# A gated linear recurrence (RG-LRU): gates computed as tanh, one logarithm per pair of tiles, element-wise work begun two projection units earlier

## The chip, the core and the metric

The kernel runs on one core of one Trainium2 chip. The metric is the device time of one execution in microseconds (us). The kernel before takes 1957.4 us, the median of three runs (1946.94 to 1958.04).

## What is computed

The program computes two blocks of a network on a sequence of 256 tokens of width 1024. The first block has two layers, each a mixer and a gated feed-forward part with norms around them; the second block (two layers of attention and delta rule) comes after and is not touched but for the name of one semaphore. The change lies in the second mixer of the first block, a gated linear recurrence of width 1280 (10 heads of 128):

```
proj = u @ w_in + b_in
ybr  = gelu(proj[:, :1280])                      # the y half
xbr  = causal_dwconv(proj[:, 1280:])             # the x half, 4 taps
gx   = sigmoid(xbr @ w_gx + b_gx)                # per head
ga   = sigmoid(xbr @ w_ga + b_ga)
log_a = -8 * softplus(-lam) * ga
a    = exp(log_a)
h_t  = a_t * h_{t-1} + sqrt(1 - a_t^2) * (gx * xbr)_t
m    = (h * ybr) @ w_out + b_out
```

## The kernel before

Everything is held transposed: features in 128 partitions, the 256 tokens along the free axis, so that a tile is 128x256. All large weights come as one stream of chunks of 128x2048 numbers (1 MB each), loaded by SyncE into a ring of three buffers `raw`. Each chunk is split before use: ScalarE copies it in two halves of 1024 columns into `w_hi` (rounded), and VectorE writes the remainder `w_lo = raw - w_hi`, also in halves. The two buffers of `w_hi` and `w_lo` alternate, so chunk c+2 can be split only while chunk c is being used up; the helper `ahead(split, engine, c)` splits chunk c+2 (`act_split` and `act_half` on ScalarE, `dve_split` and `dve_half` on VectorE). TensorE makes three products for every tile of weights (lines 521 to 523: hi with hi, hi with lo, lo with hi).

Two kinds of chunk matter here. `pe_unit` uses one of kind a: 48 matmuls that write one "unit", two output tiles, into one of the two PSUM banks `unit`. `pe_down` uses one of kind b: 48 matmuls that add a pair of input tiles (split into `mv_hi` by ScalarE, line 575, and `mv_lo` by VectorE, line 579) into the eight tiles of `acc`.

The mixer is a hand-written order of instructions on three engines, joined by semaphores. Stage `lru_in` has 10 chunks (c0 to c0+9): units 0 to 4 give the x half, units 5 to 9 the y half. Stage `lru_out` has five (c0+10 to c0+14), one "down" for each pair of tiles.

- TensorE (`pe_lru`): units 0 to 4; then five times the gate products of two heads (line 1184, into `misc`) and one more unit; then three small products (`pe_mod`, and `pe_ada` for blocks 18 and 19); then `pe_out`, the five downs. Down j waits for `mv_lo` of pair j.
- ScalarE (`act_lru`): copies units 0 to 4 out with the bias (line 1224), then per pair of heads two sigmoids each (lines 1236 and 1237) and a tanh each (line 1242, with a scale per feature), and copies out a unit of the y half (line 1248). When all gates are read it loads a table, takes the gelu of eight tiles at once (line 1252), loads the table of logarithm and exponential (line 1253), and for every pair q takes two logarithms (lines 1264 and 1265), two exponentials for a (line 1267) and `mult(q)`, the exponential of half the difference (line 1258). Since t = tanh(log a), the identity is 1 - a^2 = -2t/(1 - t): hence two logarithms. Then it loads the gelu table again, takes the gelu of the last unit from PSUM (line 1276), and makes the first two `mv_hi` (`act_lead`); `act_out` goes on with the splits and the later `mv_hi`.
- VectorE (`dve_lru`): four taps per tile of the x half (lines 1295 to 1298, each linked to the one before), the product gx*x (line 1305), `diff(q)` (line 1314, the difference of the logarithms), and `recur(q)`: sqrt(1-a^2)*gx*x (line 1321), two scans (line 1323), and the product with the y half (line 1331). `diff(0)`, `diff(1)`, a split, `recur(0)`, `diff(2)`, `recur(1)`, `diff(3)`, `diff(4)` come before the first `mv_lo`; then per down one split, one `recur`, one `mv_lo`. At the end `dve_mod`, two `dve_ada`, and the bias on the eight tiles of the result (line 1350), which the next norm reads.

GpSimd only issues DMAs in this kernel.

## Time and profile before

| | before |
|---|---|
| median of three runs | 1957.4 us |
| the profiled execution | 1948.02 us |
| its span, first to last instruction | 1945.9 us |
| mean granted TensorE clock | 0.967 |
| TensorE / VectorE / ScalarE busy | 94% / 67% / 53% |
| TensorE idle before the first down of `lru_out` | 18.25 us |

All rows below are of that one profiled execution, and times in them are from the start of its span; 2.1 us of the execution lie around the span. `lru_in` runs from 573 us to 642 us, `lru_out` from 663 us to 697 us. Busy time of TensorE counts pipelined matmuls, whose records overlap.

### The profile page before, as it was taken

The numbers are of one execution on the slowest core, as the hardware profiler recorded it, in microseconds if no ns is written. First come the engines' busy times: TensorE is split into PE (matmuls) and PEld (weight loads), VectorE is DVE, ScalarE is ACT, GpSimd is POOL, SyncE is SP. The second block draws the span as 40 slices with busy tenths as digits, with TensorE's granted clock in tenths as the row PEclk, the third lists the DMA queues.
The fourth block names the chain that finished last, engine by engine and source line by source line (L and its number), as shares of the span: only waits on it lengthen the run. The fifth ranks groups of instructions, "written<-read, shape, count | busy, mean of one in ns | idle before, by whom it ended". The sixth has DMA issues, their size and how long they took to land. (4 is left out here: it accounts for less than half of the span.)

```text
span 1945.9 us, 40030 instructions
## 1 busy us (share of the span) xinstructions
PE 1822.1 (94%) x16281; PEld 1727.0 (89%) x16281; DVE 1294.4 (67%) x1994; ACT 1026.0 (53%) x1550; POOL 29.5 (2%) x48
## 2 busy tenths in 40 slices
PE   6999999999989689999979999889998999988999
PEld 5996889999969579999969999889998999988999
DVE  5947667777657477777766866665556776766555
ACT  5644555555556655555546555344444665444443
POOL 0000000000000000000000001000000000100000
PEclk9999899999989799999989999989998999999999
DMA  7540446777754345666733340335553433044553
GB/s 287 191 154 1 170 176 247 271 260 258 269 211 159 145 173 207 225 237 226 269 108 130 135 169 24 109 109 195 195 194 124 159 133 128 3 147 141 192 193 129
DMA packets 43887, 333.54 MB, mean 171 GB/s; under 512 B 4864, under 2 KB 4992, under 8 KB 5632
## 3 DMA queue, kind: packets, MB, share of 16 engines
q1 hardware_dynamic: 38592, 277.89, 39.5%
q0 software_dynamic: 4608, 50.33, 6.9%
q10 hardware_dynamic: 576, 3.71, 0.5%
q8 instruction: 85, 1.39, 0.3%
q14 instruction: 26, 0.21, 0.0%
HBM read 330.86 MB, written 1.05 MB: 171 GB/s over the span
## 5 line engine op out<-in xcount | busy, mean ns | idle before, releaser
L501 DVE TENSOR_TENSOR w_lo<-raw,w_hi 128x1024 fp32r<-128x1024 f32 x526 | 640.5, 1224 | 435.0 <-ACT w_hi L492 425.3
L492 ACT ACTIVATE w_hi<-raw 128x1024 fp32r<-128x1024 f32 x526 | 555.4, 1061 | 615.6 <-PE unit L523 374.6
L521 PE MATMUL unit<-h_hi,w_hi 128*128 128x256 f32 x2656 | 752.7, 283 | 40.9 <-DVE h_lo L426 28.2
L522 PE MATMUL unit<-h_lo,w_hi 128*128 128x256 f32 x2656 | 745.1, 281 | 0.0
L523 PE MATMUL unit<-h_hi,w_lo 128*128 128x256 f32 x2656 | 744.9, 280 | 0.0
L521 PEld LDWEIGHTS unit<-h_hi,w_hi 128*128 128x128 f32 x2656 | 508.6, 191 | 52.5 <-issue 36.2
L522 PEld LDWEIGHTS unit<-h_lo,w_hi 128*128 128x128 f32 x2656 | 508.8, 192 | 0.2
L523 PEld LDWEIGHTS unit<-h_hi,w_lo 128*128 128x128 f32 x2656 | 508.5, 191 | 0.0
L521 PE MATMUL acc<-mv_hi,w_hi 128*128 128x256 f32 x1360 | 384.4, 283 | 33.4 <-DVE mv_lo L579 33.4
L522 PE MATMUL acc<-mv_lo,w_hi 128*128 128x256 f32 x1360 | 380.8, 280 | 0.0
L523 PE MATMUL acc<-mv_hi,w_lo 128*128 128x256 f32 x1360 | 380.6, 280 | 0.0
L521 PEld LDWEIGHTS acc<-mv_hi,w_hi 128*128 128x128 f32 x1360 | 261.0, 192 | 49.6 <-DVE mv_lo L579 35.8
L522 PEld LDWEIGHTS acc<-mv_lo,w_hi 128*128 128x128 f32 x1360 | 260.8, 192 | 0.0
L523 PEld LDWEIGHTS acc<-mv_hi,w_lo 128*128 128x128 f32 x1360 | 260.5, 192 | 0.0
L575 ACT ACTIVATE mv_hi<-keep 128x512 fp32r<-128x512 f32 x93 | 57.4, 621 | 41.0 <-DVE keep L977 13.5
L579 DVE TENSOR_TENSOR mv_lo<-keep,mv_hi 128x512 fp32r<-128x512 f32 x93 | 63.6, 687 | 14.9 <-ACT mv_hi L575 14.7
L406 PE MATMUL misc<-h,con 128*128 128x256 f32 x180 | 50.2, 440 | 19.7 <-ACT h L387 19.5
L406 PEld LDWEIGHTS misc<-h,con 128*128 128x128 f32 x180 | 39.2, 223 | 29.8 <-ACT h L387 12.9
L1035 ACT ACTIVATE keep<-unit,par 128x256 f32<-128x256 f32 x128 | 64.3, 552 | 0.0
L1089 DVE SCALAR_TENSOR_TENSOR keep<-unit,par,keep 128x254 f32<-128x254 f32 x128 | 55.8, 477 | 8.4
L1084 DVE SCALAR_TENSOR_TENSOR keep<-unit,par,keep 128x255 f32<-128x255 f32 x128 | 55.8, 477 | 5.6 <-ACT keep L1035 2.8
L1719 DVE SCALAR_TENSOR_TENSOR tmp<-unit,par,tmp 128x255 f32<-128x255 f32 (+1 forms) x96 | 41.9, 478 | 4.2 <-ACT tmp L1602 2.8
(375 smaller groups left out, 1711.1 us busy)
## 6 DMA issues: line engine op xcount, KB each, us to landing
raw<-w_in SPq DMA_DIRECT2D x263, 1024.0 KB, 4.8
ada_ring<-ada_in POOLq DMA_DIRECT2D x32, 1536.0 KB, 7.6
keep<-gates_in ACTq DMA_DIRECT2D x1, 1280.0 KB, 7.2
par<-par_in ACTq DMA_DIRECT2D x1, 1261.0 KB, 14.6
x<-x_in SPq DMA_DIRECT2D x1, 1024.0 KB, 5.6
out<-x SPq DMA_DIRECT2D x4, 256.0 KB, 2.1
con<-con_in ACTq DMA_DIRECT2D x1, 950.0 KB, 5.0
con<-con_in ACTq DMA_DIRECT2D x1, 130.0 KB, 5.8
```

Of the source, the lines that this page charges most:

```text
L406: last = mm(misc[0][:, 0:T], ones, h[:, t, :], start=(t == 2 * order[0]), stop=(t == 7))
L492: act(half(w_hi, c, k), raw[c % RAW][:, CW // 2 * k:CW // 2 * (k + 1)], ACT.Copy).then_inc(S("high_parts"), 1)
L501: tt(half(w_lo, c, k), raw[c % RAW][:, CW // 2 * k:CW // 2 * (k + 1)], half(w_hi, c, k).bitcast(f32), ALU.subtract).then_inc(S("chunk_spli ...
L521: mm(out, w, m, start=first, stop=False)
L522: mm(out, w, ml, start=False, stop=False)
L523: return mm(out, wl, m, start=False, stop=last)
L575: act(mv_hi[:, b % 2, :, :], src, ACT.Copy).then_inc(S("mv_hi_done"), 1)
L579: tt(mv_lo[:, b % 2, :, :], src, mv_hi[:, b % 2, :, :].bitcast(f32), ALU.subtract).then_inc(S("mv_ready"), 1)
L1035: ins = act(fc[:, s], unit[u % 2][:, s], ACT.Identity, bias=column(u, 4 * side + 3, i), scale=column(u, 4 * side + 2, i))
L1084: ins = stt(fc[:, o + 1:o + T], src[:, o:o + T - 1], column(u, 4 * side + 1, i), fc[:, o + 1:o + T], ALU.mult, ALU.add)
L1089: ins = stt(fc[:, o + 2:o + T], src[:, o:o + T - 2], column(u, 4 * side, i), fc[:, o + 2:o + T], ALU.mult, ALU.add)
L1719: ins = stt(dst, src[:, a:z], pr("dn_conv", 60 * l + 5 * t + tap), dst, ALU.mult, ALU.add)
```

## The change

1. TensorE issues the gate products one unit earlier: the first pair of heads after unit 3 and not after unit 4, so that two units (8 and 9) stand behind the last gate products where one stood.
2. The gates are computed as tanh(x/2) with half the bias, sigmoid being (1 + tanh(x/2))/2. VectorE makes (1 + t)*x in one instruction (line 1321 of the new kernel) and z = log a = c*t + c in another, new one (line 1324), both in the old place of the product gx*x. The factor 2 that is left over is taken back in the scale of the logarithm.
3. ScalarE takes tanh of z for a pair at once (line 1249), a = exp(z) for a pair at once (line 1253), and only one logarithm for a pair (line 1258). VectorE squares a (line 1347) and multiplies (a^2 + 1) with tanh(z) (line 1348): `square_gap(q)` in place of `diff(q)`. 1 - a^2 = -(1 + a^2)*tanh(log a).
4. No table load stands between tanh and gelu in the new program, and units 5 to 7 take their gelu while they are copied from PSUM (line 1235). Units 8 and 9 are copied plain, and one gelu over four tiles follows later (line 1299). The program has three table loads in this mixer where it had five.
5. Before the first down only pairs 0 to 2 have `square_gap`, and only `recur(0)` is done; `square_gap(3)` and `(4)` stand behind downs 0 and 1. The halves of a chunk's `w_lo` are made on either side of `mv_lo`. VectorE's split of chunk c0+15 is moved ahead of `dve_mod`.
6. Three semaphores of the second block become one (same waits).

```diff
-            for j in range(1, 5):
+            for j in range(1, 4):
                 pe_unit(pe, c0 + j, n0 + j)
...
             for k in range(5):
                 gates(2 * k)
                 gates(2 * k + 1)
-                pe_unit(pe, c0 + 5 + k, n0 + 5 + k)
+                pe_unit(pe, c0 + 4 + k, n0 + 4 + k)
+            pe_unit(pe, c0 + 9, n0 + 9)
...
+            def gate_in(n, func):
+                done_after(ac, c0 + n)
+                for e in range(2):
+                    j = 2 * (n - 5) + e
+                    ins = act(R["yb"][:, j, :], unit[n % 2][:, T * e:T * (e + 1)], func, bias=pr("lru_b_in", j))
+                ins.then_inc(S("unit_free"), 1)
...
-                    act(R["gx"][:, j % 3, :], misc[j % 2][:, 0:T], ACT.Sigmoid, bias=pr("b_gx", j))
-                    act(ga_(j)[:, 0, :], misc[j % 2][:, T:2 * T], ACT.Sigmoid,
-                        bias=pr("b_ga", j)).then_inc(S("lru_gate_read"), 1)
+                    act(R["gx"][:, j % 3, :], misc[j % 2][:, 0:T], ACT.Tanh, scale=0.5, bias=cv[0][:, j:j + 1])
+                    act(ga_(j)[:, 0, :], misc[j % 2][:, T:2 * T], ACT.Tanh, scale=0.5, bias=cv[1][:, j:j + 1]
+                        ).then_inc(S("lru_gate_read"), 1)
...
+            def tanh_z(q):
+                ac.wait_ge(S("lru_z"), 2 * q + 2)
+                act(w_(2 * q, 2), ga_(2 * q, 2), ACT.Tanh).then_inc(S("lru_tanh"), 1)
+
+            def decay(q):
+                ac.wait_ge(S("lru_tanh"), q + 1)
+                act(ga_(2 * q, 2), ga_(2 * q, 2), ACT.Exp).then_inc(S("lru_a"), 1)
+
+            def mult(q):
+                ac.wait_ge(S("lru_diff"), q + 1)
+                p = lg[:, 2 * q:2 * q + 2, :]
+                link(act(p, p, ACT.Ln, scale=-0.25, bias=one("tiny")))
+                act(p, p, ACT.Exp, scale=0.5).then_inc(S("lru_mult"), 1)
...
+            for k in range(4):
+                gates(k)
+                if k >= 1:
+                    tanh_z(k - 1)
+                ahead(act_split, ac, c0 + 4 + k)
+                if k == 0:
+                    conv_in(4)
+                else:
+                    gate_in(4 + k, ACT.Gelu_apprx_tanh)
+            gates(4)
+            tanh_z(3)
+            tanh_z(4)
             ac.preload_act_table_set(LN_EXP)
...
+            mult(0)
+            ahead(act_split, ac, c0 + 8)
+            gate_in(8, ACT.Identity)
+            moving(0)
+            mult(1)
+            gate_in(9, ACT.Identity)
+            ahead(act_split, ac, c0 + 9)
+            mult(2)
+            moving(1)
+            mult(3)
...
+            act(R["yb"][:, 6:10, :], R["yb"][:, 6:10, :], ACT.Gelu_apprx_tanh).then_inc(S("lru_gelu"), 1)
...
+            def gated(k):
+                for j in (2 * k, 2 * k + 1):
+                    dve.wait_ge(S("lru_gate_read"), j + 1)
+                    stt(R["xb"][:, j, :], R["gx"][:, j % 3, :], 1.0, R["xb"][:, j, :], ALU.add, ALU.mult
+                        ).then_inc(S("lru_gated"), 1)
+                    g = ga_(j)[:, 0, :]
+                    ts(g, g, cv[3][:, j:j + 1], cv[3][:, j:j + 1], ALU.mult, ALU.add).then_inc(S("lru_z"), 1)
...
+            def square_gap(q):
                 s = lg[:, 2 * q:2 * q + 2, :]
-                dve.wait_ge(S("lru_logs"), q + 1)
-                tt(s, s, w_(2 * q, 2), ALU.subtract).then_inc(S("lru_diff"), 1)
+                dve.wait_ge(S("lru_a"), q + 1)
+                link(tt(s, ga_(2 * q, 2), ga_(2 * q, 2), ALU.mult))
+                stt(s, s, 1.0, w_(2 * q, 2), ALU.add, ALU.mult).then_inc(S("lru_diff"), 1)
...
+            for q in range(3):
+                square_gap(q)
+            for q in range(5):
+                recur(q)
+                ahead(dve_half, dve, c0 + 8 + q, 0)
+                dve_moving(dve, B0["lru_out"] + q, lru_pair(q))
+                ahead(dve_half, dve, c0 + 8 + q, 1)
+                if q < 2:
+                    square_gap(q + 3)
+            ahead(dve_split, dve, c0 + 13)
```

The next rows are ScalarE's, from the gates of the last pair of heads to the first `mv_hi`. `misc0` and `misc1` hold the gate products of heads 8 and 9. Before:

```order
L1237 ACTIVATE keep<-misc1,par 128x256
L1242 ACTIVATE keep<-keep 128x256 x2
L1252 ACT_TABLE_LOAD
L1252 ACTIVATE keep<-keep 128x2048
L1253 ACT_TABLE_LOAD
L1264 ACTIVATE keep<-late,con 128x512
L1265 ACTIVATE late<-late,con 128x512
L1267 ACTIVATE h<-h,keep 128x256 x2
L1264 ACTIVATE keep<-late,con 128x512
L1265 ACTIVATE late<-late,con 128x512
L1267 ACTIVATE h<-h,keep 128x256 x2
L1258 ACTIVATE keep<-keep 128x512
```

and now:

```order
L1244 ACTIVATE keep<-misc1,keep 128x256
L1249 ACTIVATE late<-h 128x512
L1249 ACTIVATE keep<-keep 128x512
L1281 ACT_TABLE_LOAD
L1253 ACTIVATE h<-h 128x512 x4
L1253 ACTIVATE keep<-keep 128x512
L1258 ACTIVATE keep<-keep,con 128x512
L1259 ACTIVATE keep<-keep 128x512
L492 ACTIVATE w_hi0<-raw2 128x1024 x2
L1235 ACTIVATE keep<-unit0,par 128x256 x2
L575 ACTIVATE mv_hi<-keep 128x512
```

The gelu over eight tiles and its two table loads stood between the gates and the first logarithm; now one table load stands there, and only one logarithm, one square root and one split stand between the exponentials and the first `mv_hi`.

The next rows are VectorE's, from the end of the gates to the second `mv_lo`. `late`, `h` and `keep` hold tanh(z), a and everything else. Before:

```order
L1314 TENSOR_TENSOR keep<-keep,late 128x512 x2
L501 TENSOR_TENSOR w_lo1<-raw0,w_hi1 128x1024 x2
L1321 TENSOR_TENSOR keep<-keep 128x512
L1323 SCALAR_TENSOR_TENSOR late<-h,keep 128x256 x2
L1331 TENSOR_TENSOR keep<-late,keep 128x512
L1314 TENSOR_TENSOR keep<-keep,late 128x512
L1321 TENSOR_TENSOR keep<-keep 128x512
L1323 SCALAR_TENSOR_TENSOR late<-h,keep 128x256 x2
L1331 TENSOR_TENSOR keep<-late,keep 128x512
L1314 TENSOR_TENSOR keep<-keep,late 128x512
L1314 TENSOR_TENSOR keep<-keep 128x512
L579 TENSOR_TENSOR mv_lo<-keep,mv_hi 128x512 x2
```

and now, from the last `square_gap` ahead of `recur(0)`:

```order
L1347 TENSOR_TENSOR keep<-h 128x512
L1348 SCALAR_TENSOR_TENSOR keep<-keep,late 128x512
L1353 TENSOR_TENSOR keep<-keep 128x512
L1355 SCALAR_TENSOR_TENSOR late<-h,keep 128x256 x2
L1362 TENSOR_TENSOR keep<-late,keep 128x512
L501 TENSOR_TENSOR w_lo0<-raw2,w_hi0 128x1024
L579 TENSOR_TENSOR mv_lo<-keep,mv_hi 128x512
L501 TENSOR_TENSOR w_lo0<-raw2,w_hi0 128x1024
L1347 TENSOR_TENSOR keep<-h 128x512
L1348 SCALAR_TENSOR_TENSOR keep<-keep,late 128x512
L1353 TENSOR_TENSOR keep<-keep 128x512
L1355 SCALAR_TENSOR_TENSOR late<-h,keep 128x256 x2
```

The first `mv_lo` no longer waits for two pairs' recurrences; each later one has a whole `recur`, two half splits and, twice, a `square_gap` between it and the one before.

## Rows read from the trace of the kernel before

**Rows 1.** The page: the span and the busy time of each engine.
```profile
span 1945.9 us, 40030 instructions
...
PE 1822.1 (94%) x16281; PEld 1727.0 (89%) x16281; DVE 1294.4 (67%) x1994; ACT 1026.0 (53%) x1550; POOL 29.5 (2%) x48
```

**Rows 2.** Busy time by stretch, us from the span's start.
```profile
core 0: us, PE busy (x) PEld busy (x) DVE busy (x) ACT busy (x) POOL busy (x), PEclk, DMA share, GB/s
...
636.60:645.10 8.50, 8.50 (x88) 6.54 (x87) 1.45 (x3) 8.38 (x13) 0.53 (x1) 1.00 0.34 125
645.10:663.30 18.20, 0.01 (x1) 0.00 (x0) 11.57 (x17) 17.25 (x30) 0.53 (x1) 0.56 0.61 231
663.30:667.60 4.30, 4.25 (x20) 4.25 (x21) 0.60 (x1) 0.00 (x0) 0.00 (x0) 0.50 0.00 0
667.60:696.90 29.30, 26.37 (x222) 25.58 (x221) 22.10 (x34) 10.98 (x12) 0.00 (x0) 1.00 0.36 130
```

**Rows 3.** Timeline of PE: start, us, instruction [idle before, and what ended it].
```profile
587.56 0.36 PE L521 MATMUL unit<-h_hi,w_hi 128*128 128x256 f32 x1 [0.30 <-DVE w_lo L501]
...
593.59 0.36 PE L521 MATMUL unit<-h_hi,w_hi 128*128 128x256 f32 x1
...
605.36 1.89 PE L1184 MATMUL misc<-keep 128*128 128x256 f32 x8
...
612.74 1.89 PE L1184 MATMUL misc<-keep 128*128 128x256 f32 x8
...
634.69 1.89 PE L1184 MATMUL misc<-keep 128*128 128x256 f32 x8
...
663.35 0.58 PE L521 MATMUL acc<-mv_hi,w_hi 128*128 128x256 f32 x1 [18.25 <-DVE mv_lo L579]
...
677.76 0.38 PE L521 MATMUL acc<-mv_hi,w_hi 128*128 128x256 f32 x1 [0.91 <-DVE mv_lo L579]
...
691.16 0.38 PE L521 MATMUL acc<-mv_hi,w_hi 128*128 128x256 f32 x1 [0.99 <-DVE mv_lo L579]
```

**Rows 4.** Timeline of ACT, from the last gates to the first mv_hi.
```profile
636.57 0.48 ACT L1236 ACTIVATE keep<-misc,par 128x256 f32<-128x256 f32 x1
...
638.17 0.91 ACT L1242 ACTIVATE keep<-keep 128x256 f32<-128x256 f32 x2
639.10 1.28 ACT L1252 ACT_TABLE_LOAD   x1
640.39 1.92 ACT L1252 ACTIVATE keep<-keep 128x2048 f32<-128x2048 f32 x1
...
643.62 0.72 ACT L1264 ACTIVATE keep<-late,con 128x512 f32<-128x512 f32 x1
...
661.94 1.15 ACT L575 ACTIVATE mv_hi<-keep 128x512 fp32r<-128x512 f32 x2
```

**Rows 5.** Timeline of DVE in lru_out.
```profile
673.46 0.69 DVE L1321 TENSOR_TENSOR keep<-keep 128x512 f32<-128x512 f32 x1
...
675.49 0.69 DVE L1331 TENSOR_TENSOR keep<-late,keep 128x512 f32<-128x512 f32 x1
677.01 0.69 DVE L579 TENSOR_TENSOR mv_lo<-keep,mv_hi 128x512 fp32r<-128x512 f32 x1 [0.83 <-ACT mv_hi L575]
677.89 2.36 DVE L501 TENSOR_TENSOR w_lo<-raw,w_hi 128x1024 fp32r<-128x1024 f32 x2 [0.18 <-ACT w_hi L492]
...
693.57 0.20 DVE L1147 TENSOR_TENSOR mod<-misc,par 128x48 f32<-128x48 f32 x1
...
696.08 3.22 DVE L1350 TENSOR_SCALAR keep<-acc,par 128x256 f32<-128x256 f32 x8
```

**Rows 6.** Groups of DVE from 573 to 700 us: xcount | busy, mean ns.
```profile
L1296 DVE SCALAR_TENSOR_TENSOR keep<-keep,par 128x255 f32<-128x255 f32 x10 | 4.8, 484 | 0.4
...
L1295 DVE TENSOR_SCALAR keep<-keep,par 128x256 f32<-128x256 f32 x10 | 4.1, 409 | 3.4 <-ACT keep L1224 3.4
...
L1305 DVE TENSOR_TENSOR keep<-keep 128x256 f32<-128x256 f32 x10 | 4.2, 424 | 1.9 <-ACT h L1237 1.3 <-ACT keep L1237 0.5
```

More of the change, by code:

```diff
@@ L1214, in act_lru, with conv_in @@
             act(cv[1], cv[1], ACT.Ln, bias=one("one")).then_inc(S("lam_steps"), 1)
[L1215 removed]
+            ac.preload_act_table(ACT.Gelu_apprx_tanh)
             c0, n0 = CH0["lru_in"], U0["lru_in"]
             ac.wait_ge(S("unit_free"), n0 + 2)
[L1218 removed]
+            def conv_in(n):
                 done_after(ac, c0 + n)
@@ L1227, in act_lru, with gates @@
                 ac.sem_inc(S("unit_free"), 1)
-                ahead(act_split, ac, c0 + n)
-            ac.wait_ge(S("lam_steps"), 2)
-            for k in range(5):
+            def gate_in(n, func):
[4 more added lines that the diff above has]
+                ins.then_inc(S("unit_free"), 1)
+            def gates(k):
                 for j in (2 * k, 2 * k + 1):
@@ L1235, in act_lru @@
                         ac.wait_ge(S("lru_gated"), j - 2)
-                    act(R["gx"][:, j % 3, :], misc[j % 2][:, 0:T], ACT.Sigmoid, bias=pr("b_gx", j))
-                    act(ga_(j)[:, 0, :], misc[j % 2][:, T:2 * T], ACT.Sigmoid,
-                        bias=pr("b_ga", j)).then_inc(S("lru_gate_read"), 1)
-                ac.wait_ge(S("lru_gate_read"), 2 * k + 2)
-                for j in (2 * k, 2 * k + 1):
-                    ins = act(w_(j)[:, 0, :], ga_(j)[:, 0, :], ACT.Tanh, scale=cv[3][:, j:j + 1])
@@ L1243, in act_lru @@
-                ins.then_inc(S("lru_tanh"), 1)
-                if k < 4:
-                    ahead(act_split, ac, c0 + 5 + k)
-                    done_after(ac, c0 + 5 + k)
-                    for e in range(2):
-                        ins = act(R["yb"][:, 2 * k + e, :], unit[(k + 1) % 2][:, T * e:T * (e + 1)], ACT.Identity,
-                                  bias=pr("lru_b_in", 2 * k + e))
-                    ins.then_inc(S("unit_free"), 1)
-            ac.wait_ge(S("unit_free"), n0 + 11)
@@ L1255, in mult @@
+            def decay(q):
+                ac.wait_ge(S("lru_tanh"), q + 1)
+                act(ga_(2 * q, 2), ga_(2 * q, 2), ACT.Exp).then_inc(S("lru_a"), 1)
             def mult(q):
                 ac.wait_ge(S("lru_diff"), q + 1)
-                act(lg[:, 2 * q:2 * q + 2, :], lg[:, 2 * q:2 * q + 2, :], ACT.Exp, scale=0.5).then_inc(S("lru_mult"), 1)
-            for q in range(5):
-                w = w_(2 * q, 2)
-                ac.wait_ge(S("lru_tanh"), q + 1)
-                link(act(lg[:, 2 * q:2 * q + 2, :], w, ACT.Ln, scale=-2.0, bias=one("tiny")))
-                act(w, w, ACT.Ln, scale=-1.0, bias=one("one")).then_inc(S("lru_logs"), 1)
-                for j in (2 * q, 2 * q + 1):
-                    ins = act(ga_(j)[:, 0, :], ga_(j)[:, 0, :], ACT.Exp, scale=cv[3][:, j:j + 1])
-                ins.then_inc(S("lru_a"), 1)
-                if q >= 1:
-                    mult(q - 1)
-                if q == 1:
-                    ahead(act_split, ac, c0 + 9)
@@ L1273, in act_lru @@
-            mult(4)
-            done_after(ac, c0 + 9)
-            for e in range(2):
-                ins = act(R["yb"][:, 8 + e, :], unit[1][:, T * e:T * (e + 1)], ACT.Gelu_apprx_tanh,
-                          bias=pr("lru_b_in", 8 + e))
-            ins.then_inc(S("unit_free"), 1)
-            made = lambda j: ac.wait_ge(S("lru_out_ready"), j + 1)
-            act_lead(ac, "lru_out", lru_pair, made)
-            act_out(ac, "lru_out", lru_pair, made, all_ahead=False)
+                p = lg[:, 2 * q:2 * q + 2, :]
@@ new lines, in mult, with moving @@
+                link(act(p, p, ACT.Ln, scale=-0.25, bias=one("tiny")))
+                act(p, p, ACT.Exp, scale=0.5).then_inc(S("lru_mult"), 1)
+            def moving(j):
+                ac.wait_ge(S("lru_out_ready"), j + 1)
+                act_moving(ac, B0["lru_out"] + j, lru_pair(j))
+            for n in range(4):
+                conv_in(n)
+                ahead(act_split, ac, c0 + n)
+            ac.wait_ge(S("lam_steps"), 2)
+            for k in range(4):
[7 more added lines that the diff above has]
+                    gate_in(4 + k, ACT.Gelu_apprx_tanh)
@@ L1283, in dve_lru @@
+            done_after(ac, c0 + 10)
+            moving(2)
+            mult(4)
+            ac.wait_ge(S("unit_free"), n0 + 12)
+            act(R["yb"][:, 6:10, :], R["yb"][:, 6:10, :], ACT.Gelu_apprx_tanh).then_inc(S("lru_gelu"), 1)
+            for j in (1, 2):
+                ahead(act_split, ac, c0 + 10 + j)
+                done_after(ac, c0 + 10 + j)
+                moving(2 + j)
+            ahead(act_split, ac, c0 + 13)
+            done_after(ac, c0 + 13)
         def dve_lru(dve, link):
```

51 lines of the change are left out of this document (20 added, 31 removed).

## The prediction

> **What bounds the kernel now.** I read the page first: TensorE is busy for 1822.1 of 1945.9 us [rows 1], so time is to be had only where TensorE stands still or runs at the low clock. The busy time by stretch shows the largest such place in the mixer: from 645.1 to 663.3 us TensorE does nothing (0.01 us busy in 18.20), the granted clock falls to 0.56 there, and the next 4.3 us run at 0.50, the lower of its two levels, before it is 1.00 again [rows 2]. The timeline of TensorE gives the wait: 18.25 us before the first down, ended by `mv_lo`, and three more of about 1 us before the third, fourth and fifth down (0.91 and 0.99 are the first and the last) [rows 3]. So the last chain before 663.35 us is element-wise: gates, tanh, table load, gelu of eight tiles (1.92 us), table load, logarithms, exponentials, recurrences, `mv_hi` [rows 4].
>
> Two cadences are needed. In the first part one unit follows another every 593.59 - 587.56 = 6.03 us, of which 0.30 is a wait for `w_lo` [rows 3]; a unit is thus 5.7. A pair of gate products with one unit takes 612.74 - 605.36 = 7.38. In `lru_out` three downs start 691.16 - 677.76 = 13.40 apart, that is 6.70 each and 5.71 without the wait of 0.99 [rows 3].
>
> **Part 1, the gates one unit earlier.** Before, the last pair of gate products starts at 634.69 and ends 1.89 later, at 636.58 [rows 3]. The first pair started at 605.36, after unit 4; now it follows unit 3, one turn of 6.03 earlier, and the four turns to the last pair are the same work. So the last gate products end at 636.58 - 6.03 = 630.55. I call this t = 0. Two units and three small products stand behind it where one unit did: the stretch of 8.50 us [rows 2] plus a unit of 5.7, so TensorE is free at t = 14.2 (644.75).
>
> What could hold TensorE in this part is VectorE, whose split of chunk c0+6 now stands behind the first gates and the taps of heads 8 and 9. From the split before it, VectorE has 4 small operations (1.8), 8 taps (8 at 0.41 to 0.48, 3.9 with their links) and the split itself (2.36) [rows 5, 6]: 8.1 us, against a TensorE turn of 7.38. This happens in one turn only, the half that is wanted first is there 1.2 us before the other, and the turns before and after it need far less than 7.38. I cost it at nothing; with that cover gone each us behind is one us.
>
> **Part 2, the chain from the last gates to the first down.** ScalarE reads four gates: 638.17 - 636.57 = 1.6. VectorE then needs (1+t)x and z for the last head. The first is a two-tensor operation with a scalar, which takes 0.48 for 255 columns, the second one as the first tap, 0.41 [rows 6]: t = 2.5. Tanh of a pair, 512 columns, is not in the trace with this function; `mv_hi` of that size takes 1.15 for two, so 0.6: t = 3.1. The table load is 1.28 [rows 4]: 4.4. The first exponential of a pair is ready at 5.0 and the fifth leaves ScalarE free at 7.1. VectorE makes `square_gap` from 5.0: a product of 512 columns is 0.69 [rows 5]; the second instruction has not been seen at 512 columns. Its ends are 0.69 (as a plain product) and 0.96 (twice the 0.48). I take 0.75, the plain product with the 0.06 that separates 0.48 from the plain 0.42 of a 256-column product [rows 6]. So 1.45 a pair, 9.4 for three. ScalarE's logarithm (0.72) and exponential for pair 0 end at 8.5, hidden beside it. `recur(0)` is 675.49 - 673.46 + 0.69 = 2.72, with a hand-over 2.75 [rows 5]: 12.1. `mv_hi` lies beside the first half split (1.15, half of the 2.3 net that two halves take), then `mv_lo` 0.65: ready at t = 14.0.
>
> TensorE is free at 14.2. The two meet: the wait of 18.25 goes, and with it the slow clock: the first down starts warm.
>
> **Part 3, the five downs.** Now each `mv_lo` has one VectorE turn behind the one before: two half splits 2.3, `recur` 2.75, `mv_lo` 0.65 = 5.7, and for downs 1 and 2 a `square_gap` of 1.45 as well = 7.15. TensorE needs 5.71. Hence `mv_lo` at 14.0, 21.15, 28.3, 34.0, 39.7 and downs at 14.2, 21.15, 28.3, 34.0, 39.7: waits of 1.2 and 1.4, then none. ScalarE must keep up. Its tightest point is the new gelu, of 1024 columns (half of 1.92 and a little, about 1.06, with a load of 1.28 [rows 4]): after `mult(4)` it ends at 30.5, while `recur(3)` wants it at 31.3; a split later `mv_hi` of pair 3 is made at 33.1, with no slack left.
>
> The last down starts at 630.55 + 39.7 = 670.25, against 691.16 [rows 3]: 20.9 us earlier.
>
> **Part 4, the end of the stage.** Before, the bias of the result starts at 696.08, 4.92 after the last down [rows 3, 5]. Now VectorE has, after the last `mv_lo`, one half split (1.15), the whole split of chunk c0+15 (2.3) and the same `dve_mod` and ada steps, 696.08 - 693.57 = 2.51 [rows 5]: 5.96. That gives 1.0 back. The norm waits for this bias, so it counts.
>
> **The sum.** -20.9 + 1.0 = -19.9 us. Checked the other way: 18.25 and 2.9 of short waits go, 2.6 come; the slow clock goes (20 matmuls in the 4.3 us of [rows 2] take 2.0 more than at full clock); one wait of 0.3 in the first part goes; 1.0 is lost at the end: 18.25 + 2.9 - 2.6 + 2.0 + 0.3 - 1.0 = 19.85. The profiled execution took 1948.0, so the same execution now takes 1928.1. It lay at the lower end of the three runs shown; from the median, 1957.4, the same gain gives 1937.5. The renamed semaphore and the small product that halves the biases (ten columns each, before the first unit is done) cost nothing.
>
> **A rule on table loads.** ScalarE's table load at 639.10 begins when the tanh ends (638.17 and 0.91) and the gelu starts 1.29 later, at 640.39 [rows 4]; so a load costs its 1.28 us here and no more. The Trainium skill (ScalarE: Activation LUTs, What ACT_TABLE_LOAD costs) has 1283 ns and a drain of about 1380 ns more, 2.66 us for each switch. By that rule the first `mv_lo` would come 1.4 us later and the gelu 0.6 too late for `recur(3)`, and the sum would be some 18 us. The trace does not agree, and I go by the trace.
>
> **Rivals.**
> A. *VectorE and ScalarE stay the bound in `lru_out`.* The turn of 5.7 has no slack, and each step takes what the other engine hands over. Before, each turn held 0.83 us in which VectorE waited for `mv_hi` (676.18 to 677.01 [rows 5]). If that wait stays in the four turns, 3.3 us more are lost, and with the upper price of the unseen instruction (0.2 in five) 1 us more: gain 15.6, 1941.8. For it: one late gelu shifts all behind it. Against: the half split now lies in exactly this place.
> B. *The gap only shrinks.* ScalarE's load, the five exponentials and three `square_gap` are in series before `recur(0)`; if every hand-over costs 0.1 more than I took, some fifteen hand-overs make 1.5 us at the first down, and the split of c0+6 holds TensorE by 1 us: gain 17.4, 1940.0.
> C. *The gain comes back later.* The stream of weights would have to be short. Against: the ring holds three chunks only, so the idle 18 us stored no more than that, and the DMA engines were busy for 0.36 in the downs [rows 2]. Then a gain of 5 to 12, about 1949.
> D. *Slower: the clock falls and stays low.* TensorE changes between gate products, units and downs more tightly now, and downs 1 and 2 start after waits of 1.2 and 1.4, longer than any that the clock has stood in this stage. If it is low from t = 0 to the last down, each of the 2 x 48 matmuls of the units and the 5 x 48 of the downs costs 0.096 more (4.3 / 20 = 0.215 against 5.71 / 48 = 0.119): the first down starts at 14.2 + 9.2 = 23.4, a down takes 10.3, hiding VectorE's turns, and the last ends at 74.9, that is 705.4. Before it ended at 696.9; with what is late at the end there (the bias ends at 699.3, 2.4 after, where 0.8 would do) the stage is 7 us longer: 1964. The point from which it decides is some 19.9 / 0.096 = 207 matmuls at the low clock of these 336. Against it: three waits of 0.91 to 0.99 left the granted clock at 1.00, and it was 1.00 between units and gates [rows 2, 3]. The Trainium skill (TensorE: Matmul & The Clock Gate, A second HAM failure mode) tells of a kernel in which small idle times between groups of matmuls made the clock go up and down; no row here shows it.
>
> **Chances.** Forecast 0.62, A 0.17, B 0.11, C 0.06, D 0.04. A measurement of this kernel can tell about 1% from no change, here 19.6 us, and my gain of 19.9 lies just at that line. Of the forecast's 0.62 some 0.48 lie above it, with 0.04 from scatter in the others: faster 0.52, same 0.44, slower 0.04. The predicted time is that of the forecast, 1937.5. The runs of before lie 11 us apart, so the median can fall at either end: the low end is 1946.9 less 21.5, the high end 1958.0 less 10: 1925.5 to 1948.
>
> **What the next profile should show.** TensorE without a wait over 0.5 us between the last unit and the first down, and the granted clock at 1.00 from 600 us to the end of the downs; waits before downs 1 and 2 of 1 to 1.5 us for `mv_lo`, none over 0.3 before 3 and 4; last gate products near 630.5, last down near 670; three table loads in the mixer; each new VectorE instruction near 0.48, 0.41 and 0.75. It would be wrong if the first down waited over 2 us, if downs 3 and 4 waited as 1 and 2 do, or if units 5 to 7 waited for `w_lo`.

## The result and the profile after

The changed kernel takes 1927.7 us (median of four runs, 1923.87 to 1932.22) against 1957.7 us for the kernel before (1946.94 to 1960.78): a ratio of 0.986, 95% interval 0.981 to 0.990. A second, larger set of runs, below, gives 0.989 (0.986 to 0.993). The forecast was 1937.5 in a range of 1925.5 to 1948.0.

Whole executions of one kernel differ by some 10 us, about half of the effect. So all comparisons of the mechanism go by one stretch of the profiled execution, which I call the mixer time: from the first matmul of the first unit of `lru_in` to the first matmul of the next stage's first unit. Before it is 714.07 - 573.50 = 140.57 us, now 695.03 - 575.25 = 119.78: **20.8 us less, where 19.9 was forecast**.

The page of the changed kernel, against [rows 1]:

```profile
span 1930.3 us, 40025 instructions
...
PE 1825.2 (95%) x16281; PEld 1730.1 (90%) x16281; DVE 1299.7 (67%) x2010; ACT 1016.6 (53%) x1534; POOL 29.5 (2%) x48
```

TensorE has the same 16281 matmuls and is busy for 3.1 us more; the span is 15.6 us shorter, and its idle time 18.7 us (123.8 to 105.1). (The other 5 of the 20.8 us are lost elsewhere: 1.8 us ahead of the mixer, and some 3.5 us behind it, most of them around several norms after 1100 us. Two executions of one kernel differ there as well.) The busy time by stretch, against [rows 2]: gates and units, then two units behind the last gates, then the downs.

```profile
core 0: us, PE busy (x) PEld busy (x) DVE busy (x) ACT busy (x) POOL busy (x), PEclk, DMA share, GB/s
600.00:630.50 30.50, 30.50 (x236) 29.67 (x235) 25.47 (x44) 19.95 (x36) 0.00 (x0) 1.00 0.52 182
630.50:644.70 14.20, 14.20 (x129) 13.29 (x131) 9.86 (x16) 12.88 (x23) 0.00 (x0) 1.00 0.21 76
644.70:676.00 31.30, 29.46 (x258) 27.64 (x251) 30.49 (x43) 21.45 (x28) 1.06 (x2) 1.00 0.69 263
```

The stretch in which TensorE did nothing for 18.20 us is gone, and the granted clock is 1.00 in all three. In the downs VectorE is busy for 30.49 of 31.30 us: it is now the engine that sets the pace there. The timeline of TensorE, against [rows 3] (the last gates, the small products ahead of the first down, the only two waits among the downs, and the wait in the norm that follows):

```profile
630.40 1.89 PE L1184 MATMUL misc<-keep 128*128 128x256 f32 x8
...
644.99 1.48 PE L1412 MATMUL unit<-ada_ring,cact 128*32 128x384 f32 x16
...
652.93 0.39 PE L521 MATMUL acc<-mv_hi,w_hi 128*128 128x256 f32 x1 [0.80 <-DVE mv_lo L579]
...
659.89 0.39 PE L521 MATMUL acc<-mv_hi,w_hi 128*128 128x256 f32 x1 [1.04 <-DVE mv_lo L579]
...
678.65 1.53 PE L406 MATMUL misc<-h,con 128*128 128x256 f32 x6 [1.74 <-ACT h L387]
```

The first down starts without a wait at 646.40, as the small products end. ScalarE's chain after the gates, against [rows 4]:

```profile
634.66 0.63 ACT L1249 ACTIVATE keep<-keep 128x512 f32<-128x512 f32 x1 [0.30 <-DVE keep L1324]
635.31 1.28 ACT L1281 ACT_TABLE_LOAD   x1
636.61 2.20 ACT L1253 ACTIVATE h<-h 128x512 f32<-128x512 f32 x4
...
661.29 1.06 ACT L1299 ACTIVATE keep<-keep 128x1024 f32<-128x1024 f32 x1
...
664.16 0.62 ACT L575 ACTIVATE mv_hi<-keep 128x512 fp32r<-128x512 f32 x1
```

And VectorE's, against [rows 5]: the first `square_gap`, `recur(0)`, the first `mv_lo`; one turn between two `mv_lo`; and the end of the stage.

```profile
637.34 0.70 DVE L1347 TENSOR_TENSOR keep<-h 128x512 f32<-128x512 f32 x1 [2.71 <-ACT h L1253]
638.07 0.69 DVE L1348 SCALAR_TENSOR_TENSOR keep<-keep,late 128x512 f32<-128x512 f32 x1
...
645.23 0.69 DVE L579 TENSOR_TENSOR mv_lo<-keep,mv_hi 128x512 fp32r<-128x512 f32 x1
645.83 1.22 DVE L501 TENSOR_TENSOR w_lo<-raw,w_hi 128x1024 fp32r<-128x1024 f32 x1
646.97 0.68 DVE L1347 TENSOR_TENSOR keep<-h 128x512 f32<-128x512 f32 x1
647.69 0.69 DVE L1348 SCALAR_TENSOR_TENSOR keep<-keep,late 128x512 f32<-128x512 f32 x1
648.30 0.68 DVE L1353 TENSOR_TENSOR keep<-keep 128x512 f32<-128x512 f32 x1
649.01 1.27 DVE L1355 TENSOR_TENSOR_SCAN late<-h,keep 128x256 f32<-128x256 f32 x2
650.32 0.69 DVE L1362 TENSOR_TENSOR keep<-late,keep 128x512 f32<-128x512 f32 x1
651.05 1.22 DVE L501 TENSOR_TENSOR w_lo<-raw,w_hi 128x1024 fp32r<-128x1024 f32 x1
652.19 0.68 DVE L579 TENSOR_TENSOR mv_lo<-keep,mv_hi 128x512 fp32r<-128x512 f32 x1
...
659.16 0.68 DVE L579 TENSOR_TENSOR mv_lo<-keep,mv_hi 128x512 fp32r<-128x512 f32 x1
...
664.80 0.69 DVE L579 TENSOR_TENSOR mv_lo<-keep,mv_hi 128x512 fp32r<-128x512 f32 x1
...
670.45 0.69 DVE L579 TENSOR_TENSOR mv_lo<-keep,mv_hi 128x512 fp32r<-128x512 f32 x1
671.05 3.49 DVE L501 TENSOR_TENSOR w_lo<-raw,w_hi 128x1024 fp32r<-128x1024 f32 x3
...
676.97 1.26 DVE L1381 TENSOR_SCALAR keep<-acc,par 128x256 f32<-128x256 f32 x3
```

No row of VectorE here has an idle time in brackets after the first: from 637.34 to 674 us it goes from one instruction to the next. ScalarE always comes in time, with one tight place, the late gelu: `mv_hi` of pair 3 starts at 664.16, `mv_lo` at 664.80. The groups with the new instructions, against [rows 6]:

```profile
L1333 DVE SCALAR_TENSOR_TENSOR keep<-keep,par 128x255 f32<-128x255 f32 x10 | 4.8, 485 | 0.4
...
L1321 DVE SCALAR_TENSOR_TENSOR keep<-keep 128x256 f32<-128x256 f32 x10 | 4.2, 420 | 0.5 <-ACT h L1244 0.2 <-ACT keep L1244 0.2
...
L1324 DVE TENSOR_SCALAR h<-h,keep 128x256 f32<-128x256 f32 x8 | 3.2, 406 | 0.0
...
L1348 DVE SCALAR_TENSOR_TENSOR keep<-keep,late 128x512 f32<-128x512 f32 x4 | 2.8, 692 | 0.1
...
L1347 DVE TENSOR_TENSOR keep<-h 128x512 f32<-128x512 f32 x4 | 2.7, 687 | 2.7 <-ACT h L1253 2.7
```

### The profile page after: what moved, and what is told of

The parts are those of the page before. It is cut to its first block and busy times, and to the rows that moved or that the text cites. A ratio compares the mean times of both kernels' runs of the same rounds, so it can differ in the third digit from the quotient of the medians.

```text
span 1930.3 us, 40025 instructions
## 1 busy us (share of the span) xinstructions
PE 1825.2 (95%) x16281; PEld 1730.1 (90%) x16281; DVE 1299.7 (67%) x2010; ACT 1016.6 (53%) x1534; POOL 29.5 (2%) x48
```

## The experiments

Theory 1: the whole gain lies in the mixer, and it comes from TensorE's gap being closed by the order of the work. Its rival at first was a part of the gain elsewhere (the first runs showed 30 us, more than the mixer gave), for which the renamed semaphores are the only candidate. Then the parts are taken apart one by one; each diff shows the part of the edit that names it, and the instructions that hang on it move with it. Each mixer time below is that of one profiled execution; where the mixer's code is the same they repeat within 0.4 us (140.57 and 140.17; 119.78 and 119.79).

A part of what differs between two mixer times is TensorE's clock in the second of the two norms at the mixer's end. In the changed kernel the granted clock fell there for 3.4 us; in runs 3, 5, 6 and 7 it did not, and the same stretch of the norm takes 0.3 us less. The changed kernel and run 5:

```profile
686.24:691.55 5.31, 5.31 (x17) 4.14 (x17) 4.32 (x8) 1.89 (x3) 0.00 (x0) 0.68 0.60 257
```

```profile
686.48:691.51 5.03, 4.25 (x16) 2.71 (x16) 4.32 (x8) 1.89 (x3) 0.00 (x0) 1.00 0.64 269
```

So for these runs I also give the end of the bias, which no clock in the norm can move: 680.19 - 575.25 = 104.94 us after the first unit in the changed kernel, 104.92 in its repetition.

**1. The changed kernel again, with more runs.** No edit.

> The changed kernel as it is, for a second profile and more rounds. Between the first unit of the mixer and the first unit of the feed-forward part after it, the two profiles show 140.57 us before and 119.78 us changed, 20.8 less, while the medians of the four runs lie 30 us apart and the two profiled executions 15.8. Theory 1: all of the gain is made in the mixer, and what is over is where single executions of either kernel fall. Then this profile shows 119.8 in the mixer again (within 0.5), and the ratio over five rounds lies near 1 - 20.8/1955 = 0.989, with the difference between single runs of one kernel as large as 10. Theory 2: the change also shortens something outside the mixer by 7 to 9 us. Then the ratio stays at 0.985 to 0.986 and some other stage is shorter in both changed profiles than in both unchanged ones.

Measured: 1934.1 us (six runs, 1924.4 to 1937.5) against 1949.6 (19 runs, 1947.5 to 1963.8), ratio, taken over runs side by side, 0.989 (0.986 to 0.993); mixer 119.79. At 1950 us that ratio is 20.9 us. The 30 us of the first four runs were where single executions had fallen; the interval leaves room for 14 to 28 us, and nothing asks for a second source of gain.

**2. The kernel before with only the semaphores renamed.**

```diff
-            pe.wait_ge(S("at_lam_in"), l + 1)
-            mm(misc[0][:, 0:2], ones[0:64, :], lam8[0:64, 0:2], start=True, stop=True).then_inc(S("at_lam_ps"), 1)
+            pe.wait_ge(S("at_lam_steps"), 3 * l + 1)
+            mm(misc[0][:, 0:2], ones[0:64, :], lam8[0:64, 0:2], start=True, stop=True).then_inc(S("at_lam_steps"), 1)
```

> The kernel before with only the three semaphores of the second block made one. Theory 1 (all in the mixer): ratio 1.000 within the interval, mixer 140.6 us as before, and this second profile of an unchanged mixer shows how far the clock's low stretches move elsewhere by themselves: total low time other than the 130 us of the first profile by 10 or more. Theory 2 (the part outside the mixer comes from the second block): ratio 0.995 to 0.996, 7 to 9 us.

Measured: ratio 1.0002 (0.9981 to 1.0024), mixer 140.17. This part is worth nothing. The clock moved less than expected in sum (the mean granted clock is 0.966 against 0.967, some 3 us more at the low level and not 10), but it did move within the mixer: this execution has no low stretch in its first unit, so its first down comes 1.0 us earlier after the first unit, and then the low stretch behind the long wait lasts 5.5 us where it was 4.3. The agreement within 0.4 us is in part chance; a single difference below 1 us needs more than the mixer time to stand on.

**3. The changed kernel with the gates back after unit 4.**

```diff
-            for j in range(1, 4):
+            for j in range(1, 5):
...
-                pe_unit(pe, c0 + 4 + k, n0 + 4 + k)
-            pe_unit(pe, c0 + 9, n0 + 9)
+                pe_unit(pe, c0 + 5 + k, n0 + 5 + k)
...
```

The copies and splits on the other two engines move along, and the two half splits around the first `mv_lo` fall away, since chunk c0+10 is now split before the last gates are read.

> The changed kernel with the gate products again after unit 4 (one unit later), all else changed. My theory, that TensorE is free at 14.2 us after the last gate products and the first mv_lo ready at 14.0: with one unit fewer behind the gates TensorE is free at 8.5 and mv_lo is ready at about 13.4 (the split of c0+10 is no longer in its way), so a wait of 4.5 to 5 us before the first down comes back, and the low clock perhaps with it (0 to 2 us). Mixer 124 to 126.5, that is 4.5 to 6.5 longer than changed. Rival: the position of the gates buys little because VectorE is the bound in the downs anyway: mixer 120 to 121.5.

Measured: 1936.5 us (1929.4 to 1946.1), ratio 0.991 (0.988 to 0.994), mixer 123.91, which is 4.1 more (the end of the bias 4.4 more). The wait is in the expected band of 4.5 to 5 us, the mixer just under its lower edge of 124, and the rival's band is excluded. The timeline of TensorE, and its clock in the windows behind the wait:

```profile
651.80 0.38 PE L521 MATMUL acc<-mv_hi,w_hi 128*128 128x256 f32 x1 [4.75 <-DVE mv_lo L579]
```

```profile
651.80:656.00 4.20, 4.20 (x22) 4.20 (x23) 4.06 (x7) 4.17 (x7) 0.00 (x0) 0.59 0.86 366
656.00:680.00 24.00, 24.00 (x207) 23.68 (x206) 23.41 (x32) 16.50 (x20) 0.00 (x0) 1.00 0.45 154
```

A unit of 6 us moved costs 4.1, not 6: the wait of 4.75 comes back and the clock is low behind it, but downs 1 and 2 then wait no more, since VectorE's turns run on while TensorE is slow, and the first of them is shorter by the half split that this edit takes out.

**4. The changed kernel with all five `square_gap` ahead of `recur(0)`.**

```diff
-            for q in range(3):
+            for q in range(5):
                 square_gap(q)
...
-                if q < 2:
-                    square_gap(q + 3)
```

> The changed kernel with all five square_gap ahead of recur(0), so that none stands between the downs. My theory (VectorE's work between the last gates and the last mv_lo is one sum, wherever the square_gaps stand): the first mv_lo comes 2.7 later, so a wait of 2.2 to 2.7 before the first down, and the waits of 0.80 and 1.04 before downs 1 and 2 go: mixer within 0.8 us of 119.8. Rival (the order between the downs is what made the gain): the first down's wait adds to the others, mixer 122 to 123.

Measured: 1927.1 us, ratio 0.988 (0.984 to 0.991); mixer 120.09, 0.3 more. The mixer is as expected. One wait of 2.15 stands before the first down (2.2 to 2.7 were expected), and those of 0.80 and 1.04 are gone: two waits of together 1.84 became one. Where in VectorE's row the 2.7 us of work (four instructions of 0.69) stand makes next to no difference to the last `mv_lo`: it starts 95.4 us after the first unit, against 95.2. TensorE comes to the last down 1.0 us after that `mv_lo` is ready here, since the wait and the low clock have put it back. The granted clock fell at the end of the wait of 2.15 (the window has both):

```profile
644.00:650.00 6.00, 3.87 (x20) 3.88 (x21) 5.86 (x9) 5.69 (x10) 0.53 (x1) 0.72 0.95 356
```

**5. The changed kernel with one gelu over six tiles after the gates**, in place of gelu in the copies of units 5 to 7.

```diff
-                    gate_in(4 + k, ACT.Gelu_apprx_tanh)
+                    gate_in(4 + k, ACT.Identity)
...
+            act(R["yb"][:, 0:6, :], R["yb"][:, 0:6, :], ACT.Gelu_apprx_tanh).then_inc(S("lru_gelu"), 1)
```

> The changed kernel with units 5 to 7 copied plain and one gelu over their six tiles after the last tanh, ahead of the table load (no load is added). My theory (ScalarE's row from the last gates to the exponentials is on the path, with next to no slack: in the changed profile mv_lo is ready some 0.3 us before TensorE is free): the gelu of 1536 columns takes 1.5, the first down waits 1.1 to 1.3, and nothing makes up for it in the downs: mixer 120.9 to 121.3 us against 119.8. Rival (hidden by the two units that now stand behind the gates): 119.8, within 0.3.

Measured: mixer 120.82, 1.04 more, just under the expected 120.9 to 121.3; the three first downs wait 0.88, 1.24 and 1.23 us. The end of the bias is 1.31 later, so 0.3 of the price is hidden by the clock in the norm. The rival (hidden) is excluded.

**6. The changed kernel with two logarithms per pair** and their difference, in place of the square and (a^2 + 1)*t.

```diff
-                link(act(p, p, ACT.Ln, scale=-0.25, bias=one("tiny")))
...
+                link(act(lg[:, 2 * q:2 * q + 2, :], w, ACT.Ln, scale=-0.5, bias=one("tiny")))
+                act(w, w, ACT.Ln, scale=-1.0, bias=one("one")).then_inc(S("lru_logs"), 1)
...
```

> The changed kernel with the old two logarithms of tanh(z) on ScalarE and one difference on VectorE in place of square, product and one logarithm; order and the rest changed. My theory: ScalarE's row before the first square root grows by 2.3 to 2.5 us (three pairs with two logarithms where one stood once), so the first down waits about 2.1; but VectorE's turns for downs 1 and 2 are 0.7 shorter each, so the waits of 0.80 and 1.04 shrink to 0.1 to 0.4: mixer 120.5 to 121.3. Rival (one logarithm per pair is what made the gain): the mixer goes back by 5 us or more, to 125.

Measured: mixer 120.77, 0.99 more, as expected; the end of the bias is 1.26 later. The wait of 2.1 came in two parts: 1.44 us before the last small product, which needs the bank of unit 8, and 0.51 before the first down. The two downs behind it wait 0.53 and 0.51 us (0.1 to 0.4 were expected). VectorE saves an instruction of 0.69 in each `square_gap`, but ScalarE hands over later at the start.

**7. The changed kernel with two pairs ready before the first down**, VectorE's order of the kernel before.

```diff
+            recur(0)
+            ahead(dve_split, dve, c0 + 8)
+            recur(1)
+            square_gap(3)
+            square_gap(4)
+            for q in range(2):
+                dve_moving(dve, B0["lru_out"] + q, lru_pair(q))
...
```

> The changed kernel with the old order behind the gates: two recurrences and all square_gaps ahead of the first mv_lo, then the first two mv_lo together, and whole splits between the later ones. My theory (VectorE's work is one sum, so only the part of it that no longer lies beside a down is lost): the first down waits 4.0 to 4.6, downs 1 and 2 do not wait, downs 3 and 4 wait up to 0.9 since VectorE again waits for mv_hi, and the clock may fall for a while as in the kernel with later gates (up to 1.7): mixer 121.5 to 124.5. Rival (the two pairs first were the main cause of the 18 us): mixer 128 or more.

Measured: mixer 124.46, 4.7 more (the end of the bias 4.95), at the edge of what was expected, and the wait before the first down was 6.06, not 4.0 to 4.6: a slip in the sum, since the rows of the changed kernel give 5.9 (a `recur` of 2.7, half a split of 1.15 and two `square_gap` of together 2.7 more ahead of the first `mv_lo`, less the 0.6 by which it came before TensorE was free). No later down waits. The timeline and the window behind it:

```profile
647.67 0.58 PE L521 MATMUL acc<-mv_hi,w_hi 128*128 128x256 f32 x1 [6.06 <-DVE mv_lo L579]
```

```profile
647.60:652.00 4.40, 4.33 (x25) 4.33 (x26) 4.37 (x7) 3.43 (x4) 0.00 (x0) 0.63 1.01 431
```

This edit doesn't bring back the old order of ScalarE. In the kernel before, the first `mv_hi` stands behind all five `mult`, a table load and the last gelu, and VectorE, done with everything else, waits for it:

```profile
662.60 1.29 DVE L579 TENSOR_TENSOR mv_lo<-keep,mv_hi 128x512 fp32r<-128x512 f32 x2 [3.37 <-ACT mv_hi L575]
```

In the changed kernel `mv_hi` of pair 0 follows the first `mult`, and in run 7 it still comes ahead of the third. No run puts this back.

**8. The kernel before with the gates alone one unit earlier**, on TensorE the edit of 3 the other way round.

> The kernel before with one part of the change alone: the gates of the LRU follow unit 3 of the y units instead of unit 4, with their old arithmetic. Theory 1 (the chain from the last gates to the first mv_lo keeps its length of 26.8 us and one more unit of TensorE lies behind it): the wait before the first down falls from 18.25 to about 12.6 us and the mixer, first unit of lru_in to first unit of ffn1, takes 134 to 135 us against 140.2 to 140.6. Rival (moving the gates is worth only what it was worth on the changed kernel, 4.1 us, since VectorE's other work has to come first): 136 us or more.

Measured: mixer 140.01, only 0.2 to 0.6 less than before, and the wait is 17.56 where theory 1 had 12.6. It was wrong; the rival's band is met, but not by its reason, since VectorE is not late here. ScalarE's timeline shows why:

```profile
633.39 0.91 ACT L1253 ACTIVATE keep<-keep 128x256 f32<-128x256 f32 x2
634.72 1.06 ACT L492 ACTIVATE w_hi<-raw 128x1024 fp32r<-128x1024 f32 x1 [0.42 <-PE unit L523]
...
637.49 1.06 ACT L492 ACTIVATE w_hi<-raw 128x1024 fp32r<-128x1024 f32 x1 [1.71 <-PE unit L523]
638.45 0.82 ACT L1233 ACTIVATE keep<-unit,par 128x256 f32<-128x256 f32 x2
...
640.59 1.92 ACT L1264 ACTIVATE keep<-keep 128x2048 f32<-128x2048 f32 x1
```

The tanh ends at 634.3, 6 us earlier in the stage than before, but the gelu of eight tiles waits for the copy of unit 8 at 638.45, and unit 8 now stands behind the gates. It starts 65.95 us after the first unit, against 66.89 before. Here the move on TensorE is worth next to nothing, since one instruction between the gates and the first down still needs the last but one unit.

**9. The same, with the gelu cut:** six tiles right after the gates, the other two after `mult(4)`.

```diff
-            act(R["yb"][:, 0:8, :], R["yb"][:, 0:8, :], ACT.Gelu_apprx_tanh).then_inc(S("lru_gelu"), 1)
+            act(R["yb"][:, 0:6, :], R["yb"][:, 0:6, :], ACT.Gelu_apprx_tanh).then_inc(S("lru_gelu"), 1)
...
             mult(4)
+            act(R["yb"][:, 6:8, :], R["yb"][:, 6:8, :], ACT.Gelu_apprx_tanh).then_inc(S("lru_gelu"), 1)
```

> The kernel before with the gates one unit earlier, as in the last run, and the gelu of eight tiles cut in two: six tiles right after the gates, the tiles of unit 8 only after mult(4), beside the last unit's. The split of c0+8 and the copy of unit 8 (2.8 us of ScalarE) and VectorE's split of c0+8 now stand inside the chain to the first mv_lo. Theory 2 (the gates alone brought 0.5 us because the gelu of eight tiles waited for unit 8): the gelu now starts one unit earlier, 5.7 to 6.0 us are won at its start and about 2.5 to 3 are lost again behind it, so the wait before the first down is 15 to 15.7 us and the mixer takes 136.8 to 138.6 us against 140.2 to 140.6. Rival (something else than unit 8 holds the chain, and an earlier start of the gelu does not help): 139.8 or more.

Measured: mixer 137.18, 3.4 less than before and within the expected band; the wait is 14.62, a little under the expected 15 to 15.7. ScalarE's gelu and TensorE's first down:

```profile
635.15 1.49 ACT L1262 ACTIVATE keep<-keep 128x1536 f32<-128x1536 f32 x1
```

```profile
660.15 0.58 PE L521 MATMUL acc<-mv_hi,w_hi 128*128 128x256 f32 x1 [14.62 <-DVE mv_lo L579]
```

The gelu starts 635.15 - 574.09 = 61.06 us after the first unit: 5.83 earlier, as the theory has it. The chain behind it grew by the split and copy that are now in it.

**10. The changed kernel with 5 and 6 undone together**: the old arithmetic of the gap and the late gelu, in the new order.

> The changed kernel with two of its parts undone together: two logarithms per pair and the GELU ahead of the closing units' gates, the order of VectorE's work kept. Theory (ScalarE's savings are small beside the order, and add up: +1.0 and +1.0 singly): the mixer takes 121.6 to 122.2 us against 119.8, so about 18 us of the 20.8 are there without either. Rival (each hides behind the other, or together they make ScalarE the bound of the downs): 121.0 or less, or 123 or more.

Measured: mixer 122.47, 2.7 more, between the two bands. The prices add up all the same: at the end of the bias the two single runs lose 1.31 and 1.26 us, together 2.57, and this one 2.66. In mixer time the sum of the single prices is only 2.0, because their norms ran at the full clock and this one's, like the changed kernel's, did not. What is new here is that ScalarE reads unit 8 so late that the last small product, which uses that bank, waits 2.81 us for it, and the granted clock falls behind this wait. The first 2.2 us of the first down:

```profile
648.51:650.71 2.20, 2.20 (x14) 2.20 (x11) 2.20 (x3) 2.20 (x5) 0.53 (x1) 0.50 0.82 285
```

**11. The changed kernel with two further edits**: VectorE's split of c0+15 behind the bias, and the squares of pairs 3 and 4 on ScalarE.

```diff
+            def square(q):
+                act(lg[:, 2 * q:2 * q + 2, :], ga_(2 * q, 2), ACT.Square).then_inc(S("lru_sq"), 1)
...
-            ahead(dve_split, dve, c0 + 13)
...
+            ahead(dve_split, dve, c0 + 13)
...
```

> A version meant to be faster than changed: VectorE's split of chunk c0+15 stands behind the bias and not ahead of dve_mod, and ScalarE, not VectorE, squares a for pairs 3 and 4 (in the places where it waits for recur(0) and after unit 9). My theory: the bias starts as its banks close and ends about 2.4 to 2.7 us earlier after the last down; the waits before downs 1 and 2 (0.80 and 1.04) shrink to 0.1 to 0.4 each. Mixer 115.3 to 116.2 against 119.8, and a ratio to before of 0.986 to 0.988. Rival for the first part: the split is only moved into the next norm, where VectorE is on the path too, and the mixer gains nothing from it (118.4). Rival for the second: ScalarE's later rows slip instead, and downs 3 and 4 wait.

Measured: 1923.2 us (six runs, 1920.2 to 1932.3), ratio to before 0.985 (0.982 to 0.988); mixer 116.44, 3.3 less than the changed kernel. Both are just outside what was expected (115.3 to 116.2, and 0.986 to 0.988); the rival for the first part (118.4) is excluded. Its wait among the downs and its bias:

```profile
659.14 0.39 PE L521 MATMUL acc<-mv_hi,w_hi 128*128 128x256 f32 x1 [0.50 <-DVE mv_lo L579]
```

```profile
674.15 2.05 DVE L1389 TENSOR_SCALAR keep<-acc,par 128x256 f32<-128x256 f32 x5
```

The waits of 0.80 and 1.04 are now 0 and 0.50, and the bias starts at 674.15 - 575.89 = 98.26 after the first unit, against 101.72: 1.4 of these 3.5 us were won up to the last `mv_lo`, which is what the two squares of 0.7 took on VectorE, and 2.1 behind it, where the split stood (2.4 to 2.7 were expected). The two parts were not run one by one. In mixer time it beats both kernels. By whole executions it is better than before; its lead on the changed kernel, 3.3 us in the mixer, is less than what whole runs can tell.

**What the parts add up to.** In mixer time from 140.4, the mean of the two profiles with the old order: gates alone 140.0; with the gelu cut 137.2; with the rest of the new order, still with two logarithms and one late gelu, 122.5; with one logarithm and gelu in the copies, 119.8. So 18 of 20.8 us are there without the new algebra of the gap. In that step of 14.7 us stand the single pair before the first down, the alternation of `recur` and `mv_lo`, ScalarE's `mv_hi` right behind the first `mult`, the low clock that goes with the gap, and also the gates as tanh, which save a table load and make pairs; these were not taken apart in the old kernel. What the traces show of it: from the last gate products to the first `mv_lo` it is 28.1 us in run 9 and 17.0 in run 10, 11.1 less. On the changed kernel VectorE's order alone moves the first `mv_lo` by 6.5 us (7). In run 9 the last 3.88 us ahead of the first `mv_lo` are a wait for `mv_hi`, as the 3.37 in the kernel before. How much each gave in the old kernel is not shown.

On the changed kernel the order of the pairs by itself is worth 4.7 us (7) and the gates 4.1 (3). The single prices, 11 us with the two of 1.0, are about half of the gain. Part of the reason can be seen: once the gap is closed, what one part opens again is in part taken up by the waits of 0.80 and 1.04, which go in runs 3, 4 and 7. The rest lies in the parts that no run undid.

## Why the prediction was right, step by step

The time was inside the range, and the mechanism was the one forecast; three of its terms and a count were off.

- **Part 1, the gates one unit earlier: right, 6.04 of 6.03.** The last gate products end at 632.29, 57.04 us after the first unit; before it was 63.08. Units 5 to 7 do not wait for `w_lo`. What the prediction did not say is that in the old kernel this alone is worth next to nothing: runs 8 and 9 show that it needs the gelu cut as well.
- **Part 2, the chain to the first down: right.** From the end of the gate products to the first `mv_lo` made it is 645.83 - 632.29 = 13.5 us, forecast 14.0; TensorE starts the first down 14.1 later, forecast 14.2. The unseen instruction of 512 columns takes 0.69, the lower end of the bound of 0.69 to 0.96 and not the 0.75 chosen; (1+t)*x takes 0.42, not 0.48. Both were priced by the taps. The taps take their scalar from a tile (`par` among the inputs), the new ones an immediate 1.0, and the trace has the 0.06 only on the former: the mis-sized term is "the 0.06 that separates 0.48 from the plain 0.42". One line elsewhere in the same trace runs with either kind of scalar, and shows the same difference at 1024 columns, with `par` and without:

```profile
L1735 DVE SCALAR_TENSOR_TENSOR keep<-keep,par,h 128x1024 f32<-128x1024 f32 x4 | 5.1, 1285 | 0.4 <-DVEq L1757 0.4
L1735 DVE SCALAR_TENSOR_TENSOR keep<-keep,h 128x1024 f32<-128x1024 f32 x4 | 4.9, 1226 | 3.7 <-ACT h L1586 3.7
```

- **Part 3, the downs: right, the turns a little short.** The `mv_lo` start 6.96, 6.97, 5.64 and 5.65 apart; forecast 7.15 and 5.7. Waits 0.80 and 1.04 for 1.2 and 1.4, none after. ScalarE's tightest place held, with 0.02 us between the end of `mv_hi` and `mv_lo`. The last `mv_lo` is ready at 671.05, 38.8 us after the last gates (39.7). Here and in part 2 lie the 0.9 us by which the sum of 19.9 was too small: start to start, each of the five `square_gap` took 1.33 us for the 1.45 forecast, and each of the five `mv_lo` 0.60 for 0.65.
- **Part 4, the end: right.** The bias starts 676.97 - 671.05 = 5.9 us after the last `mv_lo` (5.96). Run 11 shows that this is time on the path: with the split of c0+15 behind the bias, that distance is 2.1 us shorter.
- **The table load: the trace's price held.** The load at 635.31 begins when tanh ends (634.66 and 0.63) and the exponential starts 1.30 after it. The 2.66 us per switch of the Trainium skill (ScalarE: Activation LUTs, What ACT_TABLE_LOAD costs) isn't seen here either. My text says three loads in the mixer where there were five; the trace has four (lines 1210, 1216, 1281 and 1299) against five. The sum had priced the right ones.
- **Rivals.** A: the wait of 0.83 for `mv_hi` in each turn did not stay; all turns are VectorE's own work. B: the first down waits for nothing. C: the next stage starts 20.8 us earlier, and run 1's ratio gives 20.9 for the whole; a loss of 10 us or more is excluded, one of a few is not. D: the granted clock stayed 1.00 behind waits of 0.80 and 1.04, in run 5 behind waits up to 1.24, and behind the 1.74 in the norm. It did fall with the waits of 4.75 and 6.06 in runs 3 and 7, as before with 18.25, in run 4 with 2.15 and in run 10 with 2.81, each time for the first 10 to 20 matmuls of the first down only. The length of the wait doesn't decide alone: behind the 2.48 in the second norm the clock fell in the changed kernel and stayed at 1.00 in runs 3, 5, 6 and 7.
- **The time itself.** 1937.5 was the median shown less 19.9. The runs of the changed kernel gave 1927.7 and then 1934.1; the difference of 6.4 between them is the same program. That the first set gave 30 us where the mixer gave 20.8 is luck, and the forecast time was closer to the second: it rests on the median of three runs, which lay 8 us above that of the 19 runs measured later (1949.6). The chance of 0.52 for faster by over 1% is borne out by a narrow margin: the first ratio is 0.986, the second, 0.989, lies just at that line.

## What to carry to other kernels

Where a fast engine waits for an element-wise chain between two stages, give it the independent work that it has, and then look for every instruction of the chain that still needs that work: one gelu over too many tiles made the whole move nearly worthless. Make only the first piece ready before the next stage starts, on every engine of the chain, and let the others follow one per turn; then the sum of the slower engine's work sets the end, and only work taken from that sum, or moved behind the stage's last result, gains more. Where two instructions of one name differ in price, look at where their scalar comes from before one prices the other.

## What was not expected

TensorE has two paces at the full granted clock. In a feed-forward part of the second block, from 1330 to 1395 us, the kernel before and its copy with renamed semaphores run the same instructions, TensorE is busy throughout and the granted clock is 1.00, yet the number of matmuls differs. Before, then the copy:

```profile
1330.00:1395.00 65.00, 65.00 (x575) 65.00 (x575) 36.35 (x36) 31.55 (x36) 0.00 (x0) 1.00 0.54 195
```

```profile
1330.00:1395.00 65.00, 65.00 (x554) 65.00 (x553) 34.77 (x36) 30.45 (x35) 0.00 (x0) 1.00 0.52 189
```

That is 0.113 against 0.117 us a matmul. Aligned matmul by matmul, the copy falls 5.8 us further behind from 1288 to 1455 us and is 8.6 behind at the end: most of the difference between the two executions. The changed kernel's profile has the quicker pace in that window and its repetition in run 1 the slower, so it is not the change. Both paces also occur within one mixer. Neither the clock nor a wait tells them apart, and what does stays open. It is one reason why a difference of a few us is read here from the mixer and the rows in it, and not from medians of whole runs.
